# Gain and shift of a layer norm taken out of the rows and given back in three places

## The chip, the cores and the metric

The kernel runs on one core of a Trainium2 chip. The metric is the device time of one execution in microseconds (us), the median of three runs.

## The reference

One layer of a streaming encoder over 2048 tokens plus 16 meta tokens, model width 1024, all in float32. The mixer is a multi-scale causal pooling; a post-norm follows it, then a SwiGLU feed-forward of width 2816, then a second norm.

```
def layer_norm(x, g, b):
    mu = mean(x);  var = mean((x - mu)**2)
    return (x - mu) * rsqrt(var + LN_EPS) * g + b

m = pool_mixer(h, a_w_in, a_w_group, a_scale, a_w_out)      # u = h @ w_in; trailing means less u; two more products
h = layer_norm(ALPHA * h + m, ln_mix_g, ln_mix_b)           # ALPHA = 2 ** 0.25
h = layer_norm(ALPHA * h + swiglu_ffn(h, ffn_w_gu, ffn_w_down), ln_ffn_g, ln_ffn_b)
```

The change is about the first of the two norms, and about `ALPHA * h` in the second line.

## The kernel before

Every matmul is done as three passes over a high and a low part of its operands: ScalarE makes the high part by a cast, VectorE the low part by a subtraction, and TensorE adds the three products in PSUM. Every semaphore wait is written by hand, and each engine works its list in the order in which it is written.

**The mixer.** Four blocks of 512 tokens (b = 0 to 3), each with four chunks of the inward product (`hidden`, line 835) and four of the outward product (`outward`, line 851), in chunks of 256 columns of weights that SP loads into `raw`. VectorE makes the trailing sums (`pool`, lines 1366 to 1382). The rows after the outward product lie in `z`, four tiles of 128 rows by 1024. `add_rows` (1400) adds the residual and takes the statistics. During the next block `aggregate` (1410) closes them, GpSimd raises the variance to the power of minus a half (`rstd_of`, 687), and `apply` (1416) on VectorE finishes the norm with two instructions for each tile, g and b of the norm lying in `gb`, spread over all partitions. For the last block (`LAST`) `aggregate` runs in unit 0 of the next stage and `apply` in its units 1 and 2. SP stores the finished rows to DRAM (`store_h`, 372, into `h_dram`).

**The turned rows.** TensorE transposes the rows (`turn_part`, 809) in block 2 and in some units from unit 5 to unit 15; ScalarE copies each turned part of 128 by 512 out of PSUM (`take_turn`, 1045), and the sums that the next stage wants are formed from these copies.

**Gate and up.** The products with `w_gu` are a seven-product scheme for two-by-two blocks (`NP` = 7): 44 units (`UNITS`, index n), each of seven `product(n, i)` of 12 matmuls (line 989). Units 0 to 21 are the first half of the tokens, 22 to 43 the second (`HALF_UNITS` = 22). Even units are gate, odd ones are up. In unit n:

- ScalarE: `unit_hi(n + 1, i)` (cast of the next unit's weights, 1160), a copy of product 0 into the bank of product 2, a copy of `bank_d` into `s5` (1277), `gate_out` (Silu, 1219), `store_a`.
- VectorE: `unit_lo(n + 1, i)` (1485), the seeding of a bank from `s5` (1580, signals `c_seeded`, for which product 4 waits), the sum of `s5` and a bank (1613, signals `c22_made`, for which product 6 waits), `up_out` (1544).
- GpSimd: in the second half, in even units, `s_forms` (four instructions of 128 by 1024, lines 750 to 755), then `unit_t123(n + 2)` and `unit_t4(n + 2)` on the weights, `up22_times_gate` in odd units, and until unit 28 the forms of the down weights (`tform`).
- SP, in this order: `load_unit(n + 2)` (443, after the last `unit_lo` of unit n), in even units of the second half `store_s` (461, after `s_forms`), `store_tform` and `load_tform`, the load of g and b of the second norm into `gb` (627, in unit 31), and in odd units `load_sa` (455), whose data the next `s_forms` wants.

Two spots of the order matter below. VectorE's list of a unit has `unit_lo(n + 1, 2)` ahead of the seeding:

```
                unit_lo(n + 1, 2)
                new_form(n, 2)

                dve.wait_ge(prod_done, NP * n + 3)
                dve.wait_ge(s5_taken, n + 1)
                ...
                nc.vector.tensor_tensor(bank(n, 2), s5[:], bank(n, 1), ALU.add).then_inc(c_seeded, 1)
```

and ScalarE's has `unit_hi(n + 1, 2)` right behind the copy into `s5`.

**Down.** 56 steps (`DSTEPS`) of the product with the down weights (1018). VectorE takes the results out of PSUM (`take`, 1643) and runs the second norm. ALPHA times the stored rows is formed there: by VectorE in `take` for t = 0, by ScalarE at t = 1 and t = 3 (1330, 1333).

## Time and profile before

| | |
|---|---|
| median of three runs | 1689.05 us (1688.55 to 1689.37) |
| the profiled execution | 1688.44 us |
| its span, first to last instruction | 1686.8 us |
| mean granted TensorE clock | 0.997 |
| TensorE busy | 1662.2 us, 99% of the span |
| VectorE busy | 977.9 us, 58% |
| GpSimd busy | 607.5 us, 36% |
| ScalarE busy | 582.6 us, 35% |
| mixer until about | 407 us |
| gate and up | 407 to 1259 us |
| down and second norm | 1259 us to the end |

Times of the rows below count from the start of the span. The execution took 1.6 us more than its span. A busy TensorE is not one at its peak, since matmuls overlap and their ends are modelled; its idle time is what can be lost or won.

### The profile page before, as it was taken

The numbers are of one execution on the slowest core, as the hardware profiler recorded it, in microseconds if no ns is written. First come the engines' busy times: TensorE is split into PE (matmuls) and PEld (weight loads), VectorE is DVE, ScalarE is ACT, GpSimd is POOL, SyncE is SP. The second block draws the span as 40 slices with busy tenths as digits, with TensorE's granted clock in tenths as the row PEclk, the third lists the DMA queues.
The fourth block names the chain that finished last, engine by engine and source line by source line (L and its number), as shares of the span: only waits on it lengthen the run. The fifth ranks groups of instructions, "written<-read, shape, count | busy, mean of one in ns | idle before, by whom it ended". The sixth has DMA issues, their size and how long they took to land.

```text
span 1686.8 us, 19005 instructions
## 1 busy us (share of the span) xinstructions
PE 1662.2 (99%) x7400; PEld 1373.8 (81%) x7400; DVE 977.9 (58%) x1056; ACT 582.6 (35%) x790; POOL 607.5 (36%) x413
## 2 busy tenths in 40 slices
PE   7999999999999999999989999999999999999998
PEld 5888888888888888888878888888888888888886
DVE  6648678788744444444645454445454443568766
ACT  5322334244333333333533333333333332332220
POOL 0000015204444665565347875666532000341002
PEclk9999999999999999999999999999999999999999
DMA  8533638654354555465445676544658443554542
GB/s 319 207 125 127 243 140 297 236 209 169 113 174 153 191 193 193 139 217 176 143 144 175 187 211 194 168 139 138 196 157 323 159 146 137 192 199 175 200 152 92
DMA packets 182265, 305.66 MB, mean 181 GB/s; under 512 B 7584, under 2 KB 131616, under 8 KB 172448
## 3 DMA queue, kind: packets, MB, share of 16 engines
q1 hardware_dynamic: 142480, 272.46, 47.8%
q10 hardware_dynamic: 37520, 23.60, 4.7%
q0 software_dynamic: 2176, 8.39, 1.3%
q8 instruction: 59, 0.97, 0.2%
q14 instruction: 30, 0.25, 0.0%
HBM read 216.86 MB, written 87.56 MB: 180 GB/s over the span
## 4 chain that ended last, share of the span: by engine, by line
PE 91%; DVE 5%; DMA 2%; issue 1%; ACT 1%; SPq 0%; POOLq 0%; POOL 0%; DVEq 0%; ACTq 0%
PE acc L989 42%; PE acc L1018 18%; PE acc L851 9%; PE acc L835 8%; PE turn L989 7%; PE turn L1018 6%; DVE split L1345 1%; DVE sums L1378 1%; DMA raw<-w_in 1%; PE acc L896 1%; DMA af_dram<-g 1%; PE turn L823 1%; DMA z<-w_group_t 0%; DVE z L1422 0%; DVE z L1417 0%
## 5 line engine op out<-in xcount | busy, mean ns | idle before, releaser
L989 PE MATMUL acc<-fb,wf 128*128 128x512 f32 x1584 | 364.6, 390 | 4.8 <-DVE g L1613 4.8
L989 PE MATMUL acc<-fa,wf 128*128 128x512 f32 x1584 | 366.2, 390 | 0.0
L989 PEld LDWEIGHTS acc<-fb,wf 128*128 128x128 f32 x1584 | 298.3, 188 | 67.4 <-issue 5.4
L989 PEld LDWEIGHTS acc<-fa,wf 128*128 128x128 f32 x1584 | 296.1, 188 | 61.2
L1018 PE MATMUL acc<-dw,da 128*128 128x512 f32 x1386 | 315.9, 389 | 0.5 <-DVE dw L1554 0.5
L1018 PEld LDWEIGHTS acc<-dw,da 128*128 128x128 f32 x1386 | 260.0, 188 | 55.3 <-DVE dw L1554 1.4
L1485 DVE TENSOR_TENSOR wf<-wt,wf 128x512 fp32r<-128x512 f32 x132 | 122.1, 926 | 182.3 <-ACT wf L1160 182.1
L1485 DVE TENSOR_TENSOR wf<-wr,wf 128x512 fp32r<-128x512 f32 x176 | 175.6, 1005 | 82.2 <-ACT wf L1160 81.7
L1160 ACT CAST wf<-wr 128x512 fp32r<-128x512 f32 x176 | 108.7, 618 | 236.7 <-PE acc L989 218.6
L685 POOL TENSOR_TENSOR wt<-wr,wt 128x512 f32<-128x512 f32 x88 | 128.7, 1462 | 141.5 <-DVE wf L1485 141.0
L851 PE MATMUL acc<-split,act_sb 128*128 128x512 f32 x768 | 176.4, 390 | 0.6 <-DVE split L1345 0.6
L835 PE MATMUL acc<-mov,split 128*128 128x512 f32 x768 | 176.9, 390 | 0.0
L851 PEld LDWEIGHTS acc<-split,act_sb 128*128 128x128 f32 x768 | 143.6, 188 | 30.7 <-issue 1.0
L835 PEld LDWEIGHTS acc<-mov,split 128*128 128x128 f32 x768 | 143.8, 188 | 29.5
L1548 DVE TENSOR_TENSOR da<-dar,da 128x1408 fp32r<-128x1408 f32 x56 | 93.0, 1661 | 118.9 <-ACT da L1241 118.9
L1241 ACT CAST da<-dar 128x1408 fp32r<-128x1408 f32 x56 | 76.8, 1372 | 183.8 <-PE acc L1018 147.7
L685 POOL TENSOR_TENSOR wt<-wr 128x512 f32<-128x512 f32 x44 | 59.8, 1360 | 155.7 <-DMA wr<-w_gu 126.2
L1018 PE MATMUL turn<-dw,da 128*128 128x512 f32 x462 | 105.9, 389 | 0.0
L1345 DVE TENSOR_TENSOR split<-raw,split 128x2048 fp32r<-128x2048 f32 x32 | 75.2, 2349 | 47.0 <-ACT split L1038 46.9
L1018 PEld LDWEIGHTS turn<-dw,da 128*128 128x128 f32 x462 | 86.7, 188 | 18.0
L1160 ACT CAST wf<-wt 128x512 fp32r<-128x512 f32 x132 | 81.9, 621 | 52.9 <-PE acc L989 37.6
L689 POOL TENSOR_TENSOR rstd<-var_eps,minus_half 128x4 f32<-128x4 f32 x4 | 7.3, 1820 | 241.5 <-DVE var_eps L1414 241.5
(108 smaller groups left out, 1637.8 us busy)
## 6 DMA issues: line engine op xcount, KB each, us to landing
wr<-w_gu SPq DMA_DIRECT2D x44, 1024.0 KB, 5.0
dar<-af_dram SPq DMA_DIRECT2D x56, 704.0 KB, 4.2
af_dram<-g ACTq DMA_DIRECT2D x33, 512.0 KB, 3.6
raw<-w_in SPq DMA_DIRECT2D x16, 1024.0 KB, 6.6
raw<-fold_dram SPq DMA_DIRECT2D x16, 1024.0 KB, 5.6
fs<-hf_dram SPq DMA_DIRECT2D x14, 1024.0 KB, 5.9
dt_raw<-w_down SPq DMA_DIRECT2D x22, 512.0 KB, 6.6
wt_dram<-dt_t SPq DMA_DIRECT2D x22, 512.0 KB, 3.9
```

What stands on the lines that cost most here:

```text
L685: return nc.gpsimd.tensor_tensor(out_, a, b, ALU.subtract)
L823: mm = nc.tensor.transpose(turn[:, slot, n * P:(n + 1) * P], pair_rows(pi, a)[:, kk * P:(kk + 1) * P], ident[:])
L835: mm = nc.tensor.matmul(acc[:, 2 * banks + m, :], w[:, a, k, m * P:(m + 1) * P], mov[:, k, v, :], start=k == 0 and n3 == 0, stop=k == KT - ...
L851: mm = nc.tensor.matmul(acc[:, OUT_BANK[half][j], :], act_sb[:, k0 + k, v, j * P:(j + 1) * P], w[:, a, k, :], start=first and k == 0 and n ...
L896: mm = nc.tensor.matmul(acc[:, 4, 0:CW], meta_s[:, k, :], w[:, a, k, :], start=k == 0 and a == 0, stop=k == KT - 1 and a == 1)
L989: mm = nc.tensor.matmul(dst, wf[:, slot, a, k, :], fa[half][i][:, v, :, k, :], start=i < 2 and k == 0 and n3 == 0, stop=k == KC - 1 and n3 ...
L1018: mm = nc.tensor.matmul(down_bank(k), da[k % 3][:, v, p, :], dw[:, slot, a, :], start=p == 0 and n3 == 0, stop=p == JF - 1 and n3 == 2)
L1160: nc.scalar.copy(wf[:, (NP * n + i) % 8, 0].rearrange("p k n -> p (k n)"), w_source(n, i)).then_inc(wf_hi, 1)
L1241: nc.scalar.copy(da[k % 3][:, 0], dar[:, k % 2]).then_inc(da_hi, 1)
L1345: nc.vector.tensor_tensor(split[:, slot, 1, 0:kn], raw[:, slot, 0:kn], f32(split[:, slot, 0, 0:kn]), ALU.subtract).then_inc(w_lo_ready, 1)
L1485: nc.vector.tensor_tensor(wf[:, s, 1].rearrange("p k n -> p (k n)"), w_source(n, i), f32(wf[:, s, 0]).rearrange("p k n -> p (k n)"), ALU.s ...
L1548: nc.vector.tensor_tensor(da[k % 3][:, 1], dar[:, k % 2], f32(da[k % 3][:, 0]), ALU.subtract).then_inc(da_lo, 1)
```

## The change

The rows in `z` and in DRAM are only normalised, (x - mu) * rstd, without g and b. ScalarE does it with one instruction for each tile (`norm`: scale rstd, bias -mu * rstd, which two more small instructions on GpSimd provide). g and b come in twice. The turned copies for the products take them as scale and bias: g and b lie by feature on the partitions there, and each `take_turn` becomes two instructions of half the width. The rows that the second norm's residual wants, all 2048 tokens, sixteen tiles of 128 rows, are loaded back from DRAM in units 30 to 37, multiplied by ALPHA * g and shifted by ALPHA * b by VectorE in units 31 to 38 (`finish_h`, two instructions a tile, two tiles a unit), and stored again in units 32 to 39. ALPHA is taken into g and b by one ScalarE instruction in unit 30, so that the multiplications by ALPHA in the down stage go. g and b of the second norm are loaded in unit 40 instead of unit 31. `TF_UNITS[-1]` is 28, so `ROW_UNIT0` is 31.

The diff, cut to its core:

```diff
+        ROW_UNIT0 = TF_UNITS[-1] + 3
...
+            def load_mgb():
+                sp.wait_ge(tf_stored, 16 * TF_STEPS)
+                for n, v in enumerate((mix_g, mix_b)):
+                    sp.dma_start(mgb[:, n, :], v.partition_broadcast(P)).then_inc(mgb_landed, 16)
+
+            def load_row(r):
+                if r == 0:
+                    sp.wait_ge(fa_lo, 2 * NP)
+                if r >= len(rows):
+                    sp.wait_ge(row_final, 16 * (r // 2 * 2 - 2))
+                n = r % len(rows)
+                sp.dma_start(rows[n][:], h_rows[:, r, :]).then_inc(row_landed[n], 16)
+
+            def store_row(r):
+                sp.wait_ge(row_ready, r + 1)
+                sp.dma_start(h_rows[:, r, :], rows[r % len(rows)][:]).then_inc(row_final, 16)
...
-            for n, v in enumerate((mix_g, mix_b)):
-                sp.dma_start(gb[:, n, :], v.partition_broadcast(P)).then_inc(gb_landed, 16)
+            for tile, v in ((mix_g_sb, mix_gt), (mix_b_sb, mix_bt)):
+                sp.dma_start(tile[:], v).then_inc(mix_gb_landed, 16)
...
 SP, unit n, behind load_unit, store_s, store_tform and load_tform:
-                if n == TF_UNITS[-1] + 3:
-                    sp.wait_ge(tf_stored, 16 * TF_STEPS)
-                    for q, v in enumerate((ffn_g, ffn_b)):
-                        sp.dma_start(gb[:, q, :], v.partition_broadcast(P)).then_inc(gb_landed, 16)
+                if n == ROW_UNIT0 - 1:
+                    load_mgb()
+                if ROW_UNIT0 + 1 <= n <= ROW_UNIT0 + MT:
+                    store_row(2 * (n - ROW_UNIT0) - 2)
+                    store_row(2 * (n - ROW_UNIT0) - 1)
+                if ROW_UNIT0 - 1 <= n < ROW_UNIT0 - 1 + MT:
+                    load_row(2 * (n - ROW_UNIT0) + 2)
+                    load_row(2 * (n - ROW_UNIT0) + 3)
...
 GpSimd, rstd_of, behind the power:
+                nc.gpsimd.tensor_tensor(mean_rstd[:], mv[:, 0:TT, 0], rstd[:, 0:TT], ALU.mult).then_inc(mean_scaled, 1)
+                pool.wait_ge(mean_scaled, s + 1)
+                sub(shift[:], zeros[:], mean_rstd[:]).then_inc(shift_ready, 1)
...
 ScalarE:
-                nc.scalar.copy(st_of(pi)[:, :, k, :], turn[:, slot, :].rearrange("p (b t) -> p b t", t=P)
-                               ).then_inc(turn_taken, 1)
+                for n, kk in enumerate((k, KC + k)):
+                    nc.scalar.activation(st_of(pi)[:, 2 * n:2 * n + 2, k, :],
+                                         turn[:, slot, 2 * n * P:2 * (n + 1) * P].rearrange("p (b t) -> p b t", t=P),
+                                         ACT.Identity, bias=mix_b_sb[:, kk:kk + 1], scale=mix_g_sb[:, kk:kk + 1]
+                                         ).then_inc(turn_taken, 1)
...
+            def norm(s, j):
+                if j == 0:
+                    act.wait_ge(shift_ready, s + 1)
+                nc.scalar.activation(z[:, j, :], z[:, j, :], ACT.Identity, bias=shift[:, j:j + 1],
+                                     scale=rstd[:, j:j + 1]).then_inc(normed, 1)
...
+                    if b:
+                        for j in ((0, 1), (2,), (3,), ())[i]:
+                            norm(b - 1, j)
...
 ScalarE, unit n, between the copy into s5 and unit_hi(n + 1, 2):
                 nc.scalar.copy(s5[:], bank_d).then_inc(s5_taken, 1)
+                if n == ROW_UNIT0 - 1:
+                    act.wait_ge(mgb_landed, 32)
+                    nc.scalar.mul(mgb[:], mgb[:], ALPHA).then_inc(mgb_scaled, 1)
+                if n in (1, 2):
+                    norm(LAST, 2 * (n - 1))
+                    norm(LAST, 2 * (n - 1) + 1)
...
 ScalarE, down stage:
-                if t == 1:
-                    act.wait_ge(hz_landed[m], 16)
-                    nc.scalar.mul(z0[:, m, 1, :], z0[:, m, 1, :], ALPHA).then_inc(h12_scaled, 1)
-                if t == 3:
-                    act.wait_ge(hs_landed[m % 2], 16 * (m // 2 + 1))
-                    nc.scalar.mul(hs[:, m % 2], hs[:, m % 2], ALPHA).then_inc(h2_scaled, 1)
...
 VectorE:
-            def apply(s, j):
-                nc.vector.scalar_tensor_tensor(out=z[:, j, :], in0=z[:, j, :], scalar=mv[:, j, 0:1], in1=gb[:, 0, :],
-                                               op0=ALU.subtract, op1=ALU.mult).then_inc(centered, 1)
...
-                nc.vector.scalar_tensor_tensor(out=z[:, j, :], in0=z[:, j, :], scalar=rstd[:, j:j + 1], in1=gb[:, 1, :],
-                                               op0=ALU.mult, op1=ALU.add).then_inc(ln_applied, 1)
...
-                        for j in ((0, 1), (), (2,), (3,))[i]:
-                            apply(b - 1, j)
...
+            def finish_h(r):
+                if r == 0:
+                    dve.wait_ge(mgb_scaled, 1)
+                n = r % len(rows)
+                dve.wait_ge(row_landed[n], 16 * (r // len(rows) + 1))
+                nc.vector.tensor_tensor(rows[n][:], rows[n][:], mgb[:, 0, :], ALU.mult).then_inc(row_gained, 1)
+                dve.wait_ge(row_gained, r + 1)
+                nc.vector.tensor_tensor(rows[n][:], rows[n][:], mgb[:, 1, :], ALU.add).then_inc(row_ready, 1)
...
 VectorE, unit n, behind unit_lo(n + 1, 3) and up_out and ahead of the sum for c22_made:
-                if n in (1, 2):
-                    apply(LAST, 2 * (n - 1))
+                if ROW_UNIT0 <= n < ROW_UNIT0 + MT:
+                    finish_h(2 * (n - ROW_UNIT0))
...
 VectorE, unit n, behind unit_lo(n + 1, 4):
-                if n in (1, 2):
-                    apply(LAST, 2 * (n - 1) + 1)
+                if ROW_UNIT0 <= n < ROW_UNIT0 + MT:
+                    finish_h(2 * (n - ROW_UNIT0) + 1)
```

## Rows read from the trace of the kernel before

**Rows 1.** The chain that ended last, the page's line by engine.

```profile
PE 91%; DVE 5%; DMA 2%; issue 1%; ACT 1%; SPq 0%; POOLq 0%; POOL 0%; DVEq 0%; ACTq 0%
```

**Rows 2.** TensorE's waits: total us, times, longest.

```profile
PE acc L989 <- DVE g L1613: 4.8, 1, 4.8
PE turn L823 <- ACT st_mix L1056: 0.9, 1, 0.9
PE acc L851 <- DVE split L1345: 0.6, 1, 0.6
```

**Rows 3.** The chain in order of time, around unit 30: start, length.

```profile
979.08 16.32 PE acc L989 x72
995.40 2.72 PE turn L989 x12
```

**Rows 4.** SP in order of time, units 30 and 31: start, time to issue.

```profile
1005.74 0.98 SPq L461 DMA_DIRECT2D af_dram<-sx  x2
1006.77 2.86 SPq L461 DMA_DIRECT2D af_dram<-sa  x2
1011.04 0.41 SPq L443 DMA_DIRECT2D wr<-w_gu  x1
1011.49 1.23 SPq L627 DMA_DIRECT2D gb<-ffn_g  x1
```

**Rows 5.** ScalarE in order of time, unit 30.

```profile
998.64 0.62 ACT L1160 CAST wf<-wt 128x512 fp32r<-128x512 f32 x1
```

**Rows 6.** VectorE in order of time, unit 30.

```profile
999.29 1.35 DVE L1485 TENSOR_TENSOR wf<-wt,wf 128x512 fp32r<-128x512 f32 x1 [1.46 <-ACT wf L1160]
1000.88 0.70 DVE L1580 TENSOR_TENSOR acc<-s,acc 128x512 f32<-128x512 f32 x1 [0.23 <-PE acc L989]
```

**Rows 7.** DMA issues by line: count, KB each, median us to landing.

```profile
sa<-af_dram SPq DMA_DIRECT2D x22, 512.0 KB, 6.1
gb<-mix_b SPq DMA_DIRECT2D x1, 512.0 KB, 11.1
gb<-ffn_b SPq DMA_DIRECT2D x1, 512.0 KB, 8.7
```

**Rows 8.** Groups of instructions, shapes apart: busy us, mean ns of one.

```profile
L1038 ACT CAST split<-raw 128x2048 fp32r<-128x2048 f32 x32 | 61.2, 1911 | 92.4 <-PE acc L851 84.6 <-DMA raw<-fold_dram 4.5 <-DMA raw<-w_in 2.7
L1417 DVE SCALAR_TENSOR_TENSOR z<-z,mv,gb 128x1024 f32<-128x1024 f32 x16 | 23.5, 1472 | 0.0
L1333 ACT ACTIVATE hs<-hs 128x1024 f32<-128x1024 f32 x8 | 8.5, 1061 | 13.7 <-DMA hs<-h_dram 13.7
```

**Rows 9.** Stretches behind unit 22's stall: length, busy by engine, PEclk, DMA share.

```profile
854.80:857.00 2.20, 2.17 (x5) 1.83 (x6) 1.29 (x3) 2.06 (x4) 0.00 (x0) 0.50 0.00 0
857.00:860.00 3.00, 3.00 (x12) 2.37 (x12) 0.59 (x1) 0.53 (x2) 1.29 (x1) 0.81 0.42 98
```

**Rows 10.** VectorE in order of time, unit 32.

```profile
1038.96 0.70 DVE L1580 TENSOR_TENSOR acc<-s,acc 128x512 f32<-128x512 f32 x1 [0.32 <-PE acc L989]
1039.66 1.78 DVE L1485 TENSOR_TENSOR wf<-wr,wf 128x512 fp32r<-128x512 f32 x1
1044.40 0.69 DVE L1613 TENSOR_TENSOR g<-s,acc 128x512 f32<-128x512 f32 x1 [2.95 <-PE acc L989]
```

**Rows 11.** GpSimd in order of time, unit 32.

```profile
1038.16 2.73 POOL L685 TENSOR_TENSOR sa<-sx,sa 128x1024 f32<-128x1024 f32 x1
1040.97 2.72 POOL L685 TENSOR_TENSOR sa<-sa 128x1024 f32<-128x1024 f32 x1
1043.66 1.29 POOL L685 TENSOR_TENSOR wt<-wr 128x512 f32<-128x512 f32 x1
```

**Rows 12.** VectorE in order of time, unit 2.

```profile
454.85 2.31 DVE L1417 SCALAR_TENSOR_TENSOR z<-z,mv,gb 128x1024 f32<-128x1024 f32 x1
457.20 2.20 DVE L1422 SCALAR_TENSOR_TENSOR z<-z,rstd,gb 128x1024 f32<-128x1024 f32 x1
```

**Rows 13.** GpSimd in order of time, unit 2.

```profile
456.04 2.27 POOL L685 TENSOR_TENSOR wt<-wr,wt 128x512 f32<-128x512 f32 x1
```

More of the change, by code:

```diff
@@ L28, with trunk @@
 NP = 7
-def trunk(nc, x, x_t, meta_t, w_in, w_group_t, scale, w_out, mix_g, mix_b, w_gu, w_down, ffn_g, ffn_b,
+def trunk(nc, x, x_t, meta_t, w_in, w_group_t, scale, w_out, mix_g, mix_b, mix_gt, mix_bt, w_gu, w_down, ffn_g, ffn_b,
           out, fold_dram, h_dram, hf_dram, af_dram, wt_dram):
@@ L132, in trunk @@
         hs = at("hs", Z0, [P, 2, D])
+        mgb = at("mgb", GB0, [P, 2, D])
+        rows = [at(f"rows{n}", off, [P, D]) for n, off in enumerate((N0, N0 + 4 * KB, V0, V0 + 4 * KB))]
         ident = sb("ident", [P, P])
         scale_sb = sb("scale_sb", [P, KT])
+        mix_g_sb = sb("mix_g_sb", [P, KT])
+        mix_b_sb = sb("mix_b_sb", [P, KT])
+        zeros = sb("zeros", [P, TT])
+        mean_rstd = sb("mean_rstd", [P, TT])
+        shift = sb("shift", [P, TT])
         stats = sb("stats", [P, 2 * MT, HALVES, 6])
@@ L170, in trunk @@
         hs_landed = [sem("hs_landed0"), sem("hs_landed1")]
+        mix_gb_landed = sem("mix_gb_landed")
+        mgb_landed = sem("mgb_landed")
+        row_landed = [sem(f"row_landed{n}") for n in range(len(rows))]
+        row_final = sem("row_final")
         out_stored = sem("out_stored")
@@ L205, in trunk @@
         rstd_ready = sem("rstd_ready")
+        zeros_ready = sem("zeros_ready")
+        mean_scaled = sem("mean_scaled")
+        shift_ready = sem("shift_ready")
+        normed = sem("normed")
+        mgb_scaled = sem("mgb_scaled")
+        row_gained = sem("row_gained")
+        row_ready = sem("row_ready")
         centered = sem("centered")
@@ L641, in _ @@
                 if n == UP_LAST - 3:
+                    sp.wait_ge(row_final, 16 * 2 * MT)
+                    for q, v in enumerate((ffn_g, ffn_b)):
+                        sp.dma_start(gb[:, q, :], v.partition_broadcast(P)).then_inc(gb_landed, 16)
                     load_dw(0, 0)
@@ L762, in _ @@
             pool.wait_ge(half_ready, 1)
+            nc.gpsimd.memset(zeros[:], 0.0).then_inc(zeros_ready, 1)
+            pool.wait_ge(zeros_ready, 1)
             rstd_of(0)
@@ L818, in turn_part @@
                 if pi < TT and part >= 2:
-                    pe.wait_ge(turn_taken, part - 1)
+                    pe.wait_ge(turn_taken, 2 * (part - 1))
                 elif pi >= TT:
-                    pe.wait_ge(turn_taken, part)
+                    pe.wait_ge(turn_taken, 2 * part)
                 for n, (a, kk) in enumerate(((1, k), (0, k), (0, KC + k), (1, KC + k))):
@@ L975, in product @@
                     if n == 0:
-                        pe.wait_ge(turn_taken, TT * TT)
+                        pe.wait_ge(turn_taken, 2 * TT * TT)
                     else:
@@ L1410, in aggregate @@
             def aggregate(s):
+                if s:
+                    dve.wait_ge(normed, s * TT)
                 for j in range(TT):
@@ L1507, in mixer_block @@
                         d_lo(b, i - 1)
-                    if not first:
-                        for j in ((0, 1), (), (2,), (3,))[i]:
-                            apply(b - 1, j)
                     if b == LAST and i >= 2:
@@ L1640, in _ @@
             up_out(2 * JF - 1, 1, bank(UP_LAST, 1))
-            dve.wait_ge(gb_landed, 64)
+            dve.wait_ge(gb_landed, 32)
+            dve.wait_ge(normed, BLOCKS * TT)
             def take(k):
@@ L1647, in take @@
                     dve.wait_ge(hz_landed[m], 16)
-                    nc.vector.scalar_tensor_tensor(out=z0[:, m, 0, :], in0=z0[:, m, 0, :], scalar=ALPHA, in1=down_bank(k),
-                                                   op0=ALU.mult, op1=ALU.add).then_inc(taken, 1)
+                    nc.vector.tensor_tensor(z0[:, m, 0, :], z0[:, m, 0, :], down_bank(k), ALU.add).then_inc(taken, 1)
                     return
@@ L1767 @@
         "mix_b": np.ascontiguousarray(inputs["ln_mix_b"][0]),
+        "mix_gt": lay(inputs["ln_mix_g"], (kt, P), (1, 0)),
+        "mix_bt": lay(inputs["ln_mix_b"], (kt, P), (1, 0)),
         "w_gu": np.ascontiguousarray(blocks(w_gu).transpose(1, 2, 3, 0, 4, 5)),
```

33 lines of the change are left out of this document (15 added, 18 removed).

## The prediction

> **What bounds the kernel now.** I read the page's chain of waits first: TensorE holds 91% of it [rows 1]. So the time moves only where TensorE stops or stops waiting, and the next view is TensorE's own waits. Behind the start, three are left: 4.8 us in unit 22, 0.9 us on a turned copy in block 2 and 0.6 us on a split in block 3 [rows 2]. That is all that relief of VectorE or ScalarE could give back. The change removes much VectorE work (16 `apply`, whose first halves alone are 23.5 us [rows 8]), but nearly all of it lies under matmuls. What has to be read closely is where the new waits stand. For that I use the chain in order of time, which gives the rhythm of a unit, and then the timelines of each engine in units 30 to 33.
>
> A product is 12 matmuls in 2.72 us, and a unit is 16.32 + 2.72 = 19.04 us; product 1 of unit 30 starts at 995.40, so unit 30 starts at 992.68 [rows 3]. Counted from a unit's start, product 4 is due at 4 x 2.72 = 10.88 and product 6 at 16.32. Unit 32 starts two units on, at 1030.76.
>
> **Part 1: the wait in unit 30.** ScalarE, behind its copy into `s5`, now waits until g and b (`mgb`) have landed. Who issues that load? SP, in its unit 30, behind `store_s`, and `store_s` waits for GpSimd's four `s_forms`. In the trace these stores are issued from 1005.74, the last pair from 1006.77 for 2.86 us, so until 1009.63 [rows 4]. The instruction that ScalarE is held from, the cast for unit 31's weights, ran at 998.64 [rows 5]. ScalarE therefore waits before its load has even been asked for. Nothing on the way to that load needs ScalarE's later work (the inputs of these `s_forms` are ready by then), so it is a stall and no deadlock.
>
> When does `mgb` land? The first load is issued at 1009.7 and the second some 1.2 us later (issue time of `gb<-ffn_g` [rows 4]), at 1010.9. A lower bound is the landing of a plain 512 KB load, 6.1 us: 1017.0. An upper bound is the slowest spread load, 11.1 us, with both issues at 1.2: 1012.3 + 11.1 = 1023.4 [rows 7]. Between them I go by the amount moved. Before, the second spread load was issued at 1011.49 + 1.23 = 1012.72 and landed 8.7 us on, at 1021.4; by then 2 MB of stores, 1 MB of weights (issued at 1011.04) and its own 1 MB had passed since 1005.74 [rows 4, 7], 4 MB in 15.7 us, 3.9 us for each. Now the weights are not ahead of it, since their load waits for VectorE's unit 31 work, which waits for ScalarE: 3 MB, some 11.8 us, 1017.5 from the same start. The issue time and the latency of a last load argue for a little more; I take 1018.6.
>
> Then ScalarE multiplies 128 by 2048 (1.95 us, by the cast of that size, 1.91 [rows 8]) and does the cast (0.62 [rows 5]), VectorE the low part `unit_lo(31, 2)` (0.69 when alone), and only then the seeding (0.70), because it stands behind `unit_lo(31, 2)` in VectorE's list [rows 6]. 1018.6 + 1.95 + 0.62 + 0.69 + 0.70 and 0.15 for hand-overs is 1022.7. Product 4 of unit 30 was due at 992.68 + 10.88 = 1003.56. TensorE stands still for **19.1 us**; the bounds are 17.5 and 23.9 us. All other engines catch up behind it.
>
> Behind the 4.8 us stall of unit 22 TensorE's granted clock was 0.50 for 2.2 us and 0.81 over the next 3.0 us [rows 9], the lower of its two levels (1.2 GHz of 2.4) for a while. That costs 2.2 x 0.50 + 3.0 x 0.19 = 1.67 us. I take **1.7 us** once, for the long stall; nothing to 1.7 us for each of the other stalls stays in the range.
>
> **Part 2: `finish_h` in units 31 to 38.** Four more VectorE instructions of 128 by 1024 a unit, both inputs in SBUF. The units that show such a load are 1 and 2, where the four of `apply` stood in these very places and TensorE did not wait. But look at how they ran. The first took 2.31 us, until 457.16; GpSimd's instruction from 456.04 ended at 458.31, 1.15 us after that; VectorE's second, from 457.20, ended at 459.40, 1.1 us after GpSimd's [rows 12, 13]. Each ran 1.1 us or so once the other was out, and stood before. In unit 32 the low part from 1039.66 ended at 1041.44, some 0.55 us after GpSimd's instruction from 1038.16 ended (1040.89), and GpSimd's next from 1040.97 ended 2.25 us after that [rows 10, 11]. So the two take turns: whichever comes second stands until the first is done.
>
> In units 1 and 2 GpSimd's instructions were short (1.3 us). In even units from 32 it runs four of 128 by 1024, some 2.35 us each without VectorE in between. Worked through for unit 32, from its start: the finishing of tiles 2 and 3 of the rows (unit 31's second `finish_h` and what follows) ends some 2.6 us later than before, so `up_out` ends at 4.4 instead of 2.0, and `s_forms` starts at 5.0. With turns of 2.35 for GpSimd, 0.6 for a low part and 1.15 for a `finish_h` instruction: GpSimd until 7.35, low part 2 until 7.95, GpSimd until 10.3, low part 3 until 10.9, GpSimd until 13.2, first `finish_h` instruction until 14.35, GpSimd until 16.7, second until 17.85. Only then comes the sum for `c22_made`, 0.70: 18.55, against 14.33 before (1044.40 + 0.69 [rows 10]). Product 6 was due at 16.32: a stall of 2.25 us. The second tile and the last low parts run 4 us into unit 33; there GpSimd has less to do, and by the same count the sum ends at 15.9, just in time. But VectorE comes 1.7 us later still into unit 34, where the sum then ends at 20.2: 3.9 us. Units 36 and 38 repeat that. Sum: 2.25 + 3 x 3.9 = **14.0 us**. The bounds are nothing, as units 1 and 2 show, and 24 us, with 5 us in each even and 1 us in each odd unit, which is what it comes to if SP's new waits make `load_sa`, and so `s_forms`, later each time.
>
> The Trainium skill (SBUF — State Buffer, section Who interferes with whom) says that a VectorE instruction with two SBUF inputs and a GpSimd instruction that reads SBUF exclude each other for the whole instruction. By it the sum is the 14 us above. If the two only slowed each other somewhat, the rows would cost next to nothing. The timelines of units 2 and 32 agree with the rule [rows 10 to 13].
>
> **Part 3: the rest.** In the mixer VectorE's trailing sums come 2.5 to 5 us earlier in blocks 2 and 3, and both small waits go: **-1.5 us** [rows 2]. ScalarE takes one `norm` a tile, 1.06 us [rows 8]; in blocks 1 to 3 it had idle time at each of these places, but if it delays `stage_u` the price is up to 1 us a block, +3 us as the other bound. In units 1 and 2 two `norm` (2.1 us) stand ahead of the cast that the seeding waits for, which ran at about 6.0 us in the unit: seeding ends near 10.5, with product 4 due at 10.88, so nothing, at worst 0.5 us a unit. Each turned copy as two halves costs some 0.2 us on ScalarE, under matmuls. The two small instructions on GpSimd, the smaller loads at the start, the down stage's dropped multiplications and the addition without ALPHA change no wait of TensorE's; the tail behind the last matmul is untouched. `gb` in unit 40 has three units to land.
>
> **Sum.** 19.1 + 1.7 + 14.0 - 1.5 = 33.3 us on the profiled execution: span 1686.8 to 1720.1, execution 1688.44 to 1721.7. The median of the runs stands 0.6 us above that execution; I predict 1722 us.
>
> **Rivals.** *The rows cost nothing* (the taking of turns is milder than worked out, as in units 1 and 2; against it stand GpSimd's long instructions in every even unit): 19.1 + 1.7 - 1.5 = 19.3, 1708 us, chance 0.26. *The waits feed each other*: SP now waits in each unit from 32 for its own row stores before it loads the next rows, and `load_unit` and `load_sa` stand behind that. `s_forms` end, 3.9 us of issuing, two row stores, about 7 us of landing, loads, the next pair with 5 us of landing, `load_sa` with 6.1 us [rows 7], and 10 us of `s_forms` add up to some 41 us for two units of 38.1. Then 24 us and three to four dips of the clock of 1.7 us stand for the rows: some 49 us in all, 1738 us, chance 0.13. *Not slower*: `mgb` would have to have landed before 1003.5 less 4.1, that is by 999.4, and the rows would have to be free; then the two waits won in the mixer are all that is left, 1687.5 us, no change that can be told. It would need the load to be issued by about 991, yet SP stands behind a store from 1005.74. Chance 0.03. My forecast (rows 6 to 20 us): 0.58.
>
> A measurement of this kernel tells about 0.2%, 3.4 us, from no change. Slower 0.96, same 0.02, faster 0.02. The range takes in the first rival and the forecast with its bounds, and ends short of the full second rival: 1706 to 1735 us.
>
> **What would show it.** In the changed profile: a wait of TensorE's in line 989 of 17 to 24 us in unit 30, whose chain goes back over VectorE's low part and ScalarE's multiplication to the DMA of `mgb`; a granted clock of 0.50 behind it; in units 32, 34, 36 and 38 waits of 2 to 4 us for the sum that makes `c22_made`, and none in the odd ones; `finish_h` instructions of about 2.3 to 3.5 us beside GpSimd; no waits left in blocks 2 and 3. The prediction is wrong if the load of `mgb` is issued before 1005, or if the even units show no waits.

## The result and the profile after

The change makes the kernel slower: 1723.36 us, the median of five runs (1723.0 to 1725.94), against 1689.05 us (1688.48 to 1689.72, five runs of before beside them). The ratio is 1.0207, 95% interval 1.0196 to 1.0219. The profiled execution took 1725.94 us and its span is 1724.1 us, at a mean granted clock of 0.988.

The page's chain that ended last, by engine, has other releasers in it than [rows 1]:

```profile
PE 83%; DMA 6%; DVE 3%; POOL 3%; issue 2%; SPq 2%; ACT 1%; POOLq 0%; DVEq 0%; ACTq 0%
```

TensorE's share fell from 91% to 83%, DMA's rose from 2% to 6%, and GpSimd and SP came in. TensorE's waits after (total, times, longest), whose counterpart is [rows 2]:

```profile
PE acc L1041 <- DVE acc L1644: 22.4, 4, 18.6
PE acc L1041 <- DVE g L1677: 12.2, 5, 4.7
...
PE acc L1041 <- DVE up L1677: 1.9, 1, 1.9
```

Line 1041 is the product of gate and up (989 before), 1644 the seeding (1580), 1677 the sum for `c22_made` (1613). The 4.7 in the second row is unit 22's old stall; the two small waits of blocks 2 and 3 are gone. In order of time, with the wait in brackets, TensorE's runs of matmuls behind a wait (a run of 24 takes 5.7 us at the full clock, one of 48 takes 11.1):

```profile
1022.90 12.92 PE L1041 MATMUL acc<-fb,wf 128*128 128x512 f32 x48 [18.60 <-DVE acc L1644]
...
1070.17 5.69 PE L1041 MATMUL acc<-fb,wf 128*128 128x512 f32 x24 [1.71 <-DVE g L1677]
1110.72 7.31 PE L1041 MATMUL acc<-fb,wf 128*128 128x512 f32 x24 [2.22 <-DVE g L1677]
1152.22 5.68 PE L1041 MATMUL acc<-fb,wf 128*128 128x512 f32 x24 [1.55 <-DVE g L1677]
1166.89 5.73 PE L1041 MATMUL acc<-fb,wf 128*128 128x512 f32 x24 [0.83 <-DVE acc L1644]
1174.53 5.72 PE L1041 MATMUL acc<-fb,wf 128*128 128x512 f32 x24 [1.91 <-DVE up L1677]
1195.85 5.72 PE L1041 MATMUL acc<-fb,wf 128*128 128x512 f32 x24 [2.00 <-DVE g L1677]
1210.52 11.13 PE L1041 MATMUL acc<-fb,wf 128*128 128x512 f32 x48 [0.79 <-DVE acc L1644]
1270.39 11.14 PE L1041 MATMUL acc<-fb,wf 128*128 128x512 f32 x48 [2.19 <-DVE acc L1644]
```

These stand in units 30, 32, 34, 36, 37, 37, 38, 39 and 42. Adding them up beside the starts of the units (unit 30 + k starts at 992.68 + 19.04 k before) gives this balance of the profiled execution:

| where | us | of it waits |
|---|---|---|
| start of unit 30 | +0.7 | |
| unit 30 | +20.6 | 18.6 |
| units 32 to 40 | +14.8 | 11.0 |
| unit 42 | +2.4 | 2.2 |
| down stage | -1.3 | |
| span | +37.3 | |

The first line holds three things. A run of 48 matmuls at 38.59 took 13.58 us, against 11.22 before and 11.1 to 11.9 in eleven of the twelve other profiles of this study (13.39 in run 11), so these 2.4 us don't come from the change. The mixer behind it won 2.0: the product stage starts at 407.23, against 406.87 before and 403.6 to 405.7 in the eleven profiles in which those matmuls were not delayed. And units 0 to 29 took 0.4 us more. The profiled execution was 2.6 us above the median of its five, that of before 0.6 below its own; that fits with a median that rose by 34.3 us where the span rose by 37.3.

Of the 1.3 us in the down stage, 1.1 stand at two waits of before that none of the other profiles has: 0.17 and 0.38 us for the low part of the down weights, where the steps from 1498.43 took 46.0 us for 198 matmuls and now take 44.9. Which of the dropped multiplications by ALPHA made them go was not tried.

**Unit 30.** SP in order of time, as [rows 4]; then ScalarE and VectorE there, as [rows 5, 6]:

```profile
1006.11 0.99 SPq L480 DMA_DIRECT2D af_dram<-sx  x2
1007.14 2.88 SPq L480 DMA_DIRECT2D af_dram<-sa  x2
1010.06 1.76 SPq L514 DMA_DIRECT2D mgb<-mix_g  x1
1011.87 1.23 SPq L514 DMA_DIRECT2D mgb<-mix_b  x1
```

```profile
1019.01 1.91 ACT L1347 ACTIVATE mgb<-mgb 128x2048 f32<-128x2048 f32 x1 [19.52 <-DMA mgb<-mix_b]
1020.82 0.60 ACT L1216 CAST wf<-wt 128x512 fp32r<-128x512 f32 x1
```

```profile
1021.46 0.69 DVE L1543 TENSOR_TENSOR wf<-wt,wf 128x512 fp32r<-128x512 f32 x1 [22.54 <-ACT wf L1216]
1022.07 0.69 DVE L1644 TENSOR_TENSOR acc<-s,acc 128x512 f32<-128x512 f32 x1
```

The load is asked for at 1010.06 and 1011.87 and has landed at 1018.99. ScalarE had stood for 19.52 us with the cast behind it, VectorE for 22.54 us on that cast with the seeding behind it, and TensorE on the seeding. The windows behind the stall, as [rows 9], show the clock at its lower level of 1.2 GHz:

```profile
1022.90:1025.00 2.10, 2.10 (x5) 1.71 (x6) 1.15 (x1) 0.05 (x1) 0.60 (x1) 0.50 0.00 0
1025.00:1027.00 2.00, 2.00 (x6) 1.58 (x6) 0.00 (x0) 0.00 (x0) 0.00 (x0) 0.56 0.00 0
```

**Unit 32**, which starts at 1052.14: VectorE, then GpSimd, as [rows 10, 11].

```profile
1061.58 2.28 DVE L1543 TENSOR_TENSOR wf<-wr,wf 128x512 fp32r<-128x512 f32 x1
1063.78 3.42 DVE L1606 TENSOR_TENSOR rows<-rows,mgb 128x1024 f32<-128x1024 f32 x1
1067.23 2.19 DVE L1608 TENSOR_TENSOR rows<-rows,mgb 128x1024 f32<-128x1024 f32 x1
1069.35 0.68 DVE L1677 TENSOR_TENSOR g<-s,acc 128x512 f32<-128x512 f32 x1
```

```profile
1055.31 2.40 POOL L800 TENSOR_TENSOR sx<-g 128x1024 f32<-128x1024 f32 x1
...
1063.39 2.73 POOL L729 TENSOR_TENSOR sa<-sa 128x1024 f32<-128x1024 f32 x1
1066.08 2.26 POOL L729 TENSOR_TENSOR wt<-wr 128x512 f32<-128x512 f32 x1
```

The first `finish_h` instruction comes 0.4 us behind GpSimd's from 1063.39, which ends at 1066.12; it ends 1.08 us after that. GpSimd's next, ready at 1066.08, ends 1.14 us after VectorE's. They take turns, as forecast. The two instructions took 5.6 us, against 1.22 us each alone (run 12), and these 3.2 us more make the sum late: it ends 17.9 us into the unit, would by this count have ended at 14.7, and product 6 is due at 16.32.

**Later even units.** GpSimd's first instruction of `s_forms` in units 34, 36 and 38:

```profile
1099.93 2.83 POOL L800 TENSOR_TENSOR sx<-g 128x1024 f32<-128x1024 f32 x1 [1.73 <-DMA sa<-af_dram]
1145.65 3.26 POOL L800 TENSOR_TENSOR sx<-g 128x1024 f32<-128x1024 f32 x1 [4.27 <-DMA sa<-af_dram]
1190.04 2.52 POOL L800 TENSOR_TENSOR sx<-g 128x1024 f32<-128x1024 f32 x1 [4.99 <-DMA sa<-af_dram]
```

It now waits for the load of `sa`, a DMA, and comes 7.8, 11.3 and 12.5 us into its unit. The forecast had this only in a rival.

### The profile page after: what moved, and what is told of

The parts are those of the page before. It is cut to its first block, busy times and chain, and to the rows that moved or that the text cites. A ratio compares the mean times of both kernels' runs of the same rounds, so it can differ in the third digit from the quotient of the medians.

```text
span 1724.1 us, 19082 instructions
## 1 busy us (share of the span) xinstructions
PE 1669.0 (97%) x7400; PEld 1377.7 (80%) x7400; DVE 993.1 (58%) x1056; ACT 603.2 (35%) x823; POOL 610.8 (35%) x422
## 2 busy tenths in 40 slices
DMA packets 187162, 322.46 MB, mean 187 GB/s; under 512 B 8384, under 2 KB 132416, under 8 KB 177344
## 4 chain that ended last, share of the span: by engine, by line
PE 83%; DMA 6%; DVE 3%; POOL 3%; issue 2%; SPq 2%; ACT 1%; POOLq 0%; DVEq 0%; ACTq 0%
PE acc L1041 32%; PE acc L1070 18%; PE acc L887 10%; PE acc L903 10%; PE turn L1070 6%; PE turn L1041 5%; DMA h_dram<-rows 2%; DMA wr<-w_gu 1%; DVE wf L1543 1%; DMA sa<-af_dram 1%; POOL sa L729 1%; PE turn L875 1%; DVE rows L1606 1%; SPq L480 1%; POOL sx L800 1%
## 5 line engine op out<-in xcount | busy, mean ns | idle before, releaser
L1041 PE MATMUL acc<-fb,wf 128*128 128x512 f32 x1584 | 371.2, 394 | 36.5 <-DVE acc L1644 22.4
L1543 DVE TENSOR_TENSOR wf<-wt,wf 128x512 fp32r<-128x512 f32 x132 | 129.4, 984 | 185.9 <-ACT wf L1216 185.6
L1543 DVE TENSOR_TENSOR wf<-wr,wf 128x512 fp32r<-128x512 f32 x176 | 179.7, 1028 | 73.6 <-ACT wf L1216 73.2
L729 POOL TENSOR_TENSOR wt<-wr 128x512 f32<-128x512 f32 x44 | 64.2, 1460 | 175.9 <-DMA wr<-w_gu 119.2
L1090 ACT CAST split<-raw 128x2048 fp32r<-128x2048 f32 x32 | 61.2, 1912 | 94.8 <-PE acc L903 91.5
```

Of the source, the lines that this page charges most:

```text
L729: return nc.gpsimd.tensor_tensor(out_, a, b, ALU.subtract)
L1041: mm = nc.tensor.matmul(dst, wf[:, slot, a, k, :], fa[half][i][:, v, :, k, :], start=i < 2 and k == 0 and n3 == 0, stop=k == KC - 1 and n3 ...
L1090: nc.scalar.copy(split[:, slot, 0, 0:kn], raw[:, slot, 0:kn]).then_inc(w_hi_ready, 1)
L1543: nc.vector.tensor_tensor(wf[:, s, 1].rearrange("p k n -> p (k n)"), w_source(n, i), f32(wf[:, s, 0]).rearrange("p k n -> p (k n)"), ALU.s ...
```

## The experiments

Every kernel was timed against before, in three rounds or five; times are medians and the intervals are 95%. The medians of before beside them lie between 1688.25 and 1689.06 us, so that a difference of under 1 us between two of the kernels tells nothing. Lines may be shifted by a few in the edited kernels.

**1. No rows at all.** `load_mgb`, the row loads and stores, ScalarE's scaling and `finish_h` are left out.

```diff
-                if n == ROW_UNIT0 - 1:
-                    load_mgb()
-                    store_row(...); load_row(...)
-                    nc.scalar.mul(mgb[:], mgb[:], ALPHA).then_inc(mgb_scaled, 1)
-                    finish_h(2 * (n - ROW_UNIT0)) ...
```

> Leaves out the loading, finishing and storing of the sixteen row tiles and the loads and scaling of the first norm's g and b in unit 30, so that the second norm's residual misses ALPHA, g and b. What stays is the norm on ScalarE, the turned copies with scale and bias, and g and b of the second norm loaded in unit 40. My account: the whole loss stands in the row work. Two waits in the mixer are won (1.5 us), and unit 42 keeps a wait of about 2 us if the load in unit 40 alone brings it; so 1687 to 1691 us, 1690 likeliest, and no wait in units 30 to 39. Rival: the move of the norm to ScalarE costs several us by itself (delayed copies out of PSUM in the mixer); then over 1692 us, with waits in blocks 1 to 3.

Measured: 1687.13 us, ratio 0.9989 (0.998 to 0.9998). So all that is lost lies in the rows and in `mgb`; all that stays of the change wins 1.8 us together (0.3 to 3.4 by the interval). In its profile the product stage starts 1.8 us earlier than before, the 44 units take 1.0 us more and the down stage 1.1 us less. The only new wait is 0.77 us, in unit 42. The kernels below are compared with this one, 1687.1.

**2. The scaling one unit later.** ScalarE multiplies `mgb` in unit 31, behind its cast for product 3, with nothing of the next seeding behind it.

```diff
-                if n == ROW_UNIT0 - 1:
-                    act.wait_ge(mgb_landed, 32)
-                    nc.scalar.mul(mgb[:], mgb[:], ALPHA).then_inc(mgb_scaled, 1)
...
                     unit_hi(n + 1, 3)
+                    if n == ROW_UNIT0:
+                        act.wait_ge(mgb_landed, 32)
+                        nc.scalar.mul(mgb[:], mgb[:], ALPHA).then_inc(mgb_scaled, 1)
```

> Changed kernel, with only ScalarE's wait for g and b and its multiplication by ALPHA moved from unit 30, behind the copy into s5, to unit 31, behind the cast of part 3. The loads stay where they are. My account: the wait of 18.6 us in unit 30 and the lower clock behind it (about 2 us) go, the row units keep their 11 us of waits and some 3 us of clock, so 1702 to 1704 us. Rival: that wait only hid others (the row units then start at once and lose more, since nothing caught up before them), so that less than half of 20 us comes back: over 1712 us.

Measured: 1707.61 us, 1.0112 (1.0099 to 1.0126). The wait of unit 30 and the low clock behind it are gone, but 15.8 us come back and not 20.6: waits of 1.36 and 2.63 us now stand in unit 32, 1.30 and 2.63 in 34, 3.70 in 36 and 2.44 in 38, and 1.40 in 42. So the result lies between the account and its rival. The long stall had given the other engines and the loads time to catch up, and so hid some 5 us of what the rows cost: `s_forms` now start 5.7 us into unit 32 and not 3.2, and that unit alone loses 6.1 us against 2.0 in the kernel after.

**3. The load earlier, the scaling where it was.** `load_mgb` moves ahead of `store_s` in SP's unit 30.

```diff
+                if n == ROW_UNIT0 - 1:
+                    load_mgb()
                 if n % 2 == 0 and jj - 1 >= JF:
                     store_s(jj - 1 - JF)
...
-                if n == ROW_UNIT0 - 1:
-                    load_mgb()
```

> Changed kernel, with only SP's load of g and b put ahead of store_s in unit 30, so that it is issued at about 994 instead of 1010. ScalarE's wait stays where it is. If the wait is the late issue: landing at about 1002, then 1.9 + 0.6 + 0.7 + 0.7 us to the seeding, 1006 against a due time of 1004.3; 2 us of wait in unit 30 instead of 18.6 and 1706 to 1709 us. Rival: the spread load itself is slow there (over 15 us to landing), and the wait shrinks by less than half.

Measured: 1709.07 us (1705.13 to 1714.12), 1.0122 (1.0104 to 1.0141); the wait in unit 30 is 3.10 us. One place in SP's list takes 15.5 of the 18.6 us away: the late issue was the cause, as read from [rows 4].

**All kernels from here on keep the scaling of run 2**, and runs 4 to 9 take the rows' own cost of 20.5 us (1707.6 - 1687.1) apart.

**4. VectorE's work alone.** The rows are loaded for the first units only and never stored; `finish_h` runs in full on what lies there.

```diff
-                if ROW_UNIT0 + 1 <= n <= ROW_UNIT0 + MT:
-                    store_row(2 * (n - ROW_UNIT0) - 2)
-                    store_row(2 * (n - ROW_UNIT0) - 1)
-                if ROW_UNIT0 - 1 <= n < ROW_UNIT0 - 1 + MT:
+                if n in (ROW_UNIT0 - 1, ROW_UNIT0):
                     load_row(...)
... the waits for loads and stores that are gone become waits for VectorE's own rows
```

> As late_scale, but the row tiles are loaded only four times and never stored; VectorE does all its 32 instructions, on the same four tiles (the residual of the second norm keeps rows without g and b). It tells VectorE and GpSimd taking turns from SP's waits and the traffic. My account: in even units the two instructions ahead of the sum for c22_made still push it past its due time, 1.5 to 2.3 us a unit, so 7 to 10 us over no_rows, 1697 to 1700 us; the waits in units 37 and 39, which come from loads that SP issues late, go. Rival: all of it is traffic and SP's waits; then within 2 us of no_rows.

Measured: 1699.4 us, 1.0065 (1.005 to 1.0081), 12.3 us over no rows, as expected, with waits for the sum in units 32, 34, 36 and 38 (2.63, 2.04, 2.05 and 2.05 us), one of 1.38 us for the seeding in unit 32, and none in the odd ones:

```profile
1049.30 5.69 PE L1038 MATMUL acc<-fb,wf 128*128 128x512 f32 x24 [2.63 <-DVE g L1677]
...
1130.09 5.72 PE L1038 MATMUL acc<-fb,wf 128*128 128x512 f32 x24 [2.05 <-DVE g L1677]
```

**5. The traffic alone.** All loads and stores stay, but `finish_h` works on 32 of the 1024 columns (the other columns of the rows are stored as they were).

```diff
-nc.vector.tensor_tensor(rows[n][:], rows[n][:], mgb[:, 0, :], ALU.mult)
+nc.vector.tensor_tensor(rows[n][:, 0:32], rows[n][:, 0:32], mgb[:, 0, 0:32], ALU.mult)
... the addition of mgb[:, 1] likewise
```

> As late_scale, with all loads, stores and waits of the row tiles, but VectorE's 32 instructions only 32 elements wide (the rows get ALPHA, g and b in 32 of 1024 columns). It is the counterpart of the run with VectorE's work alone, which cost 12.3 us over the kernel without rows; both together cost 20.5 us. My account: SP's waits for its row stores and the weights that land late behind them cost something by themselves, but less than the 8 us that are left over, since the lateness hurts only together with a busy VectorE: 2 to 6 us over no_rows, 1689 to 1693 us. Rival: the two costs just add: 8 us over, 1695 us.

Measured: 1702.49 us, 1.0084 (1.007 to 1.0098), 15.4 us over no rows. That is a miss for my theory and more than its rival gave: what SP does for the rows costs, alone, more than VectorE's work alone.

**6. The same with one input.** The short instructions become `tensor_scalar`, without `mgb`, to tell the traffic from VectorE's turns behind GpSimd.

```diff
-nc.vector.tensor_tensor(rows[n][:], rows[n][:], mgb[:, 0, :], ALU.mult)
+nc.vector.tensor_scalar(rows[n][:, 0:32], rows[n][:, 0:32], ALPHA, None, ALU.mult)
... the addition likewise, of a constant
```

> As the run with all row traffic and narrow VectorE instructions (32 columns of the rows only), but each of these has a single SBUF input (a scalar instead of g and b), so that it need not take turns with GpSimd. That run was to leave SP's waits and the traffic alone and did not: its narrow instructions took 1.2 to 2.4 us beside GpSimd and 0.19 us alone. If taking turns is what they cost, they take 0.2 us everywhere now, the waits on the sum in unit 36 and 38 shrink by 1 to 2 us, and what is left is SP and traffic: 1693 to 1699 us. Rival: the waits come from late weights and late sa alone; no change, 1702 us.

Measured: 1702.31 us (1696.6 to 1703.08), 1.0067 (1.0047 to 1.0087). The form of the instruction changes nothing in the time, and it didn't take the turns away either: one of these still took up to 2.38 us beside GpSimd, 0.18 in the median. So this run could not tell the two apart; run 7 does. The waits in line 1041 are 0.23 and 5.10 us in unit 36, 2.09 in 38 and 2.11 in 42. The chain that ends at unit 36's late `s_forms` shows whose they are (start, length):

```profile
1076.30 2.38 POOL sx L800
...
1090.81 1.78 SPq L526
...
1092.64 5.97 DMA h_dram<-rows
...
1100.54 10.20 DMA h_dram<-rows
1110.75 0.32 SPq L522
...
1112.06 10.02 DMA sa<-af_dram
...
1122.31 2.35 POOL sx L800
```

It is a loop: `s_forms`, its stores, two row stores whose landing SP waits for before `load_row`, one more pair of stores and a wait of 10.2 us more, only then `load_sa`, and the next `s_forms`. It takes 1122.31 - 1076.30 = 46.0 us, and two units without waits take 38.1. The unit's weights stand behind the same waits:

```profile
1107.97 1.30 POOL L729 TENSOR_TENSOR wt<-wr 128x512 f32<-128x512 f32 x1 [14.71 <-DMA wr<-w_gu]
```

**7. The turns alone.** The edits of runs 4 and 5 together, whose diffs stand there: no traffic, 32 columns.

> As the run with VectorE's row work on four tiles and no row traffic (1699.4 us), but its 32 instructions 32 elements wide instead of 1024, both inputs still in SBUF. If an instruction of VectorE costs mostly the turn that it gives to GpSimd, and little by its own length, most of its 12.3 us over the kernel without rows stay: 7 to 12 us, 1694 to 1699 us. If the length of the instruction costs, under 5 us over: below 1692 us.

Measured: 1686.59 us, 0.9987 (0.9977 to 0.9996), as without rows. The first instruction of a tile still took 1.3 us in the mean, up to 2.4, by standing behind GpSimd's, against 0.19 alone; so these turns by themselves cost TensorE nothing, and the 12.3 us of run 4 need the instructions' full length as well. That is the second of the expectation's two cases. Full-length instructions without turns were not run.

**8. SP's order, without VectorE's length.** One input and 32 columns as in run 6, all the traffic, and SP's list rearranged: the row stores ahead of `store_s`, the row loads behind `load_sa`.

```diff
+                if ROW_UNIT0 + 1 <= n <= ROW_UNIT0 + MT:
+                    store_row(...)          # both
                 if n % 2 == 0 and jj - 1 >= JF:
                     store_s(jj - 1 - JF)
...
-                    store_row(...); load_row(...)
...
                 if half and n % 2 == 1:
                     load_sa(jj - JF)
+                if ROW_UNIT0 - 1 <= n < ROW_UNIT0 - 1 + MT:
+                    load_row(...)           # both
```

> As one_input (short one-input instructions on 32 columns in finish_h, all the traffic of the rows, the scaling of mgb late), with SP's order of sp_order: the row stores ahead of store_s, the row loads behind load_sa. Theory, SP's waits make load_sa and the weights late: then the 15 us that one_input lost against no_rows (1687.1) come back, 1687 to 1692 us, and no wait of over 1.5 us is left in units 32 to 43. Rival, the rows' 16 MB through DRAM cost it by sharing the queues, whatever the order: 1697 to 1703, waits of 2 to 5 us in units 36 and 38 as in one_input. Between 1692 and 1697: both have a part.

Measured: 1686.83 us (1685.52 to 1687.75, ten runs), 0.9991 (0.9981 to 1.0). All 15 us are back, with every byte still moved (322.46 MB in both profiles). `s_forms` starts every 38.1 us, released by VectorE again:

```profile
1069.84 2.40 POOL L800 TENSOR_TENSOR sx<-g 128x1024 f32<-128x1024 f32 x1 [1.58 <-DVE g L1599]
1107.92 2.40 POOL L800 TENSOR_TENSOR sx<-g 128x1024 f32<-128x1024 f32 x1 [1.66 <-DVE g L1599]
1146.04 2.40 POOL L800 TENSOR_TENSOR sx<-g 128x1024 f32<-128x1024 f32 x1 [1.22 <-DVE g L1599]
```

SP's waits for its own row stores fell from 42.5 us to 11.7 over the kernel. It was the place of the rows' issues and waits in SP's list, and not the bytes.

**9. SP's order, with the full `finish_h`.** The diff of run 8 for SP's list, on the kernel of run 2 with `finish_h` unchanged.

> As late_scale, with SP's list of a unit from 32 on changed: row stores ahead of store_s, row loads behind load_sa, so that no load of weights or of sa stands behind a wait for a row store just issued. My account: the VectorE part stays (12.3 us over no_rows) and most of the other 8 us goes: 1700 to 1703 us, with waits on c22_made of about 2 us in even units and none in unit 37. Rival: the 8 us are the traffic itself (16 MB more in 8 units) and stay: over 1705 us.

Measured: 1702.59 us, 1.0082 (1.0069 to 1.0096). 5.0 us of run 2's 20.5 come back. The waits for the sum stay (2.63, 2.65, 2.19 and 2.05 us, of which unit 36's was 3.70); the seeding waits of units 34 and 42 (1.30 and 1.40) are gone, that of unit 32 (1.33) stays.

**10. Both tiles behind the sum.** On run 2, the first `finish_h` of a unit moves behind the sum for `c22_made` and `unit_lo(n + 1, 4)`.

```diff
-                if ROW_UNIT0 <= n < ROW_UNIT0 + MT:
-                    finish_h(2 * (n - ROW_UNIT0))
...
+                    finish_h(2 * (n - ROW_UNIT0))
                     finish_h(2 * (n - ROW_UNIT0) + 1)
```

> As late_scale, with both finish_h of a unit behind the sum for c22_made and the low part 4, none ahead of it. If what costs is that two contended instructions stand ahead of a sum that TensorE waits for, the waits on c22_made in units 32 to 38 go (some 11 of 15 us) and 1694 to 1699 us are left, with waits on the seeding where the four instructions run on into the next unit. Rival: the shared access of VectorE and GpSimd is full in these units and the place does not matter: over 1704 us.

Measured: 1710.36 us (1706.02 to 1712.43), 1.0123 (1.0107 to 1.0138). A miss: no wait for the sum is left, but the next seeding is late instead, by 2.67, 3.46, 3.90 and 2.45 us in units 32, 34, 36 and 38 (and by 0.43 and 1.40 in 39 and 42). This is what its rival gave.

**11. The best of these.** The edits of runs 2, 9 and 10, and `gb` loaded in unit 42.

```diff
-                if n == UP_LAST - 3:
+                if n == UP_LAST - 1:
                     sp.wait_ge(row_final, 16 * 2 * MT)
                     for q, v in enumerate((ffn_g, ffn_b)):
```

> late_scale, behind and sp_order together, and g and b of the second norm loaded in unit 42 instead of 40. All work of the reference is done. If the three causes are the ones named (the late wait, the place of the rows' instructions, SP's order), little is left: 1687 to 1691 us, no change against the kernel before that can be told, with the two waits in the mixer won. Rival: VectorE and GpSimd together fill their shared access, and 5 us or more stay whatever the order: over 1693 us.

Measured: 1701.34 us (1697.51 to 1702.86), 1.0069 (1.0056 to 1.0082). Another miss: the seeding waits 2.99, 2.81, 1.58 and 3.25 us in the even units. No version that does all of the work came below before; this one is the fastest of them, 12.3 us slower by the medians.

**12. Four tiles in each odd unit, none in the even ones**, where GpSimd's long instructions run; SP loads and stores four rows at a time in the even units (loads in 30 to 36, stores in 32 to 38), and `gb` in unit 42.

```diff
-                if ROW_UNIT0 <= n < ROW_UNIT0 + MT:
+                if ROW_UNIT0 <= n < ROW_UNIT0 + MT and not gate:
                     finish_h(2 * (n - ROW_UNIT0))
...
-                if ROW_UNIT0 <= n < ROW_UNIT0 + MT:
-                    finish_h(2 * (n - ROW_UNIT0) + 1)
+                if ROW_UNIT0 <= n < ROW_UNIT0 + MT and not gate:
+                    for r in range(1, 4):
+                        finish_h(2 * (n - ROW_UNIT0) + r)
```

> All work of the reference. As late_scale, but the sixteen rows are finished in the odd units 31, 33, 35 and 37, four each, one ahead of the sum for c22_made and three behind it, where GpSimd has only 8 of 19 us of work instead of 16; stores and loads of rows are issued by SP in even units only; g and b of the second norm in unit 42. If the even units' turns with GpSimd's long instructions are the cause, their waits on c22_made go and some waits on the seeding in even units are left, as VectorE runs over by 4 us: 1692 to 1698 us. Rival: the run-over makes s_forms late and the next even unit pays the same: over 1700 us.

Measured: 1719.97 us, 1.0182 (1.0167 to 1.0197), the slowest of the twelve. VectorE around the start of unit 34:

```profile
1081.68 1.22 DVE L1607 TENSOR_TENSOR rows<-rows,mgb 128x1024 f32<-128x1024 f32 x1
1082.93 1.23 DVE L1609 TENSOR_TENSOR rows<-rows,mgb 128x1024 f32<-128x1024 f32 x1
...
1088.36 4.98 DVE L1544 TENSOR_TENSOR wf<-wt,wf 128x512 fp32r<-128x512 f32 x2 [1.20 <-ACT wf L1217]
1093.27 0.68 DVE L1645 TENSOR_TENSOR acc<-s,acc 128x512 f32<-128x512 f32 x1
```

Alone they take 1.22 us each, the bare cost. But `unit_lo` of the next unit stands behind six of them, GpSimd waits 9.01 us for it, `s_forms` start 9.8 us into unit 34, and `unit_lo` falls on them there: seeding waits of 6.51, 5.31, 5.93 and 5.92 us in the even units. The rival had named this.

## Why the prediction was right, and where its reasons were not

**The size.** 1722 us were predicted, 1723.4 measured. By its terms, in the profiled execution:

| term | predicted | measured |
|---|---|---|
| wait in unit 30 | 19.1 | 18.6 |
| clock behind it | 1.7 | 2.0 |
| the rows, units 32 to 40 | 14.0 | 14.8 (11.0 waits, the rest mostly clock) |
| mixer | -1.5 | -2.0 |
| unit 42 | 0 | 2.4 |
| down stage | 0 | -1.3 |
| the matmuls at 38.59 (2.4), units 0 to 29 (0.4) | 0 | 2.8 |
| sum | 33.3 | 37.3 |

The last row but one is mostly a delay of this execution. Of what the change did, two terms were put at nothing and half cancel: unit 42 and the down stage. So the median came within 1.4 us of the forecast in part by luck.

**Part 1 held in every step.** The issue (1009.7 forecast, 1010.06), the landing (1018.6 forecast, 1018.99) and the hand-over by cast, low part and seeding came as worked out; runs 2 and 3 show the cause from both sides, the place of ScalarE's wait and the place of SP's load. (One of its bounds has a slip: two issues of 1.2 us from 1009.7 give 1012.1 and not 1012.3, so the upper bound of the wait is 23.7 us.) What it left out is that a stall also hides: 4.8 of its 20.6 us came back as row waits when it went (run 2).

**Part 2 was right in size and half right in cause.** Its unit 32 was close: `s_forms` starts 3.2 us into the unit, not 5.0, the sum ends 17.9 us into it (18.55), the wait is 1.71 us (2.25); from the start of `s_forms` to the end of the sum it took 14.7 us, not 13.55, so the early start covered turns that were longer than worked out. The taking of turns is seen there and, alone, gives waits for the sum of 2.0 to 2.6 us in the four even units and none in the odd ones (run 4), with a total of 12.3 us. But two steps failed.

First, "3 x 3.9" for units 34, 36 and 38. I carried VectorE's lateness from one pair of units to the next; run 4 shows no growth (2.04, 2.05, 2.05 behind unit 32's 2.63): `s_forms` start 3.5 us into each of the three, since VectorE catches up in the odd unit.

Second, the chance of 0.13 for the rival in which the waits feed each other, and with it "none in the odd ones". Its mechanism is at work, and waits of 0.83 and 1.91 us stand in unit 37 and of 0.79 in unit 39. I made its loop 41 us, though the terms that I named add up to 32; among them were 5 us for the landing of the second pair of row stores and 6.1 for `load_sa`. Run 6 has 10.2 and 10.0 in their places. A row store took 7.6 us in the median of the profile after, and from the `s_forms` of one even unit to those of the next it takes 44.4 to 45.7 us there, and not 38.1. Its price was wrong, too: 24 us and three to four dips of the clock for the rows, some 30 in all, against 20.5 with nothing to hide them (run 2). With SP's order and VectorE's length each taken or left, in us over no rows:

| | SP as changed | SP rearranged | no traffic |
|---|---|---|---|
| `finish_h` full | 20.5 (run 2) | 15.5 (run 9) | 12.3 (run 4) |
| `finish_h` of 32 columns | 15.2 (run 6) | -0.3 (run 8) | -0.5 (run 7) |

(Runs 6 and 8 have one input, run 7 two.) The two causes don't add: 12.3 and 15.2 alone give 20.5 together. That a wait for one covers lateness of the other would explain it; this is argued, not shown. My 14 us for turns alone agreed with what both causes cost, less what the stall in unit 30 hid, by luck and not by its working. The last 3.2 us, between 12.3 and 15.5, come with the traffic under a full `finish_h`; whether by contention or by what is left of SP's waits was not told apart.

**"`gb` in unit 40 has three units to land"** was the wrong question. It landed in time; the weights of unit 43 did not, because their load stands behind it. SP and VectorE in the kernel after:

```profile
1238.14 2.05 SPq L685 DMA_DIRECT2D gb<-ffn_g  x1
...
1244.20 0.45 SPq L462 DMA_DIRECT2D wr<-w_gu  x1
```

```profile
1257.20 1.29 POOL L729 TENSOR_TENSOR wt<-wr 128x512 f32<-128x512 f32 x1 [16.23 <-DMA wr<-w_gu]
```

```profile
1263.93 5.71 DVE L1543 TENSOR_TENSOR wf<-wt,wf 128x512 fp32r<-128x512 f32 x2 [4.28 <-ACT wf L1216]
```

GpSimd gets the weights at 1257.20, just as unit 42 starts (1257.32), and so starts `s_forms` at 1263.92, 6.6 us into the unit; VectorE's low parts for the seeding then stand against these long instructions. The seeding of unit 42 follows 2.2 us late. The later `s_forms` start in this unit, the longer the wait: 2.65 us into it and no wait before, 4.5 and none in run 9, 4.9 and 0.48 in run 8, 5.1 and 0.77 in run 1, 5.8 and 1.40 in run 2, all but before with `gb` in unit 40. With `gb` in unit 42 (runs 11 and 12) no wait stands there. So without the rows `gb` costs 0.8 us there, and the rest comes with the lateness that the rows bring.

**The rivals.** "The rows cost nothing" is out: 20.5 us when nothing hides them. "Not slower" needed `mgb` before 999.4; it came at 1018.99. Freed of the rows, the change wins 1.8 us (run 1), about what was forecast for the mixer; the mixer did win 1.8 us there, and what the units lose (1.0) the down stage gives back (1.1).

The Trainium skill (DMA: Bandwidth & Descriptors, section Anatomy of one DMA — SWDGE (gpsimd) path) says that DMA engines don't wait on semaphores: the wait happens on the issuing engine before dispatch. Runs 6 and 8, whose DMAs SP issues, agree: one wait for a landing held up every load behind it in SP's list, for up to 10.0 us, and moving the rows' issues and waits in that list was worth 15.5 us.

## What to carry to other kernels

Work that comes back through DRAM has two prices, one on the engine that does it and one on the queue that issues it. Price the second by walking the issuing engine's list around a whole loop, with store landings read from under load, and put loads that feed the bound engine ahead of any wait for a store. Before moving work off a crowded place, ask what stands behind it in the same list: here the instructions ahead of the sum made the sum late, and both places behind it (runs 10 and 12) made the next seeding late instead.
